# A two-block transformer kernel on one core: the order of the first loads, the place of the bias table, and four PSUM banks for the attention probabilities

## The reference

```
cs = silu(c)
mod = (cs @ ada_w[l] + ada_b[l]).reshape(B, 3, 3, D)            # shift, scale, gate
h = rmsnorm(x, norm_g[l, 0]) * (1 + mod[:, 0, 1]) + mod[:, 0, 0]
x = x + 0.5 * mod[:, 0, 2] * swiglu(h, w_gate[l, 0], w_up[l, 0], w_down[l, 0])
h = rmsnorm(x, norm_g[l, 1]) * (1 + mod[:, 1, 1]) + mod[:, 1, 0]
x = x + mod[:, 1, 2] * mixer(h, ...)
h = rmsnorm(x, norm_g[l, 2]) * (1 + mod[:, 2, 1]) + mod[:, 2, 0]
x = x + 0.5 * mod[:, 2, 2] * swiglu(h, ...)
```

```
logits = where(mask, q @ k.T * 64 ** -0.5 + bias, -1e30)
m = max(logits); p = exp(logits - m); s = sum(p)
o_g = p @ v / s ; lse_g = m + log(s)
o = sum_g softmax_g(lse)[g] * o_g
```

## Time and profile before

| | us |
|---|---|
| median of 3 runs | 3438.85 |
| lowest, highest | 3420.95, 3454.4 |
| the profiled execution's own time | 3429.66 |
| its span | 3427.9 |

### The profile page before, as it was taken

The page is one execution under the profiler, slowest core; times in us unless marked ns, Lnnn a source line. Parts: engine busy times, 40 slices in busy tenths (PEclk is TensorE's granted clock), DMA queues, the critical chain, the costliest instruction groups (busy, mean ns, idle before and its releaser), DMA issues.

```text
span 3427.9 us, 56270 instructions
## 1 busy us (share of the span) xinstructions
PE 3193.9 (93%) x24082; PEld 2691.2 (79%) x24083; DVE 1022.8 (30%) x2204; ACT 473.2 (14%) x1077; POOL 15.1 (0%) x26
## 2 busy tenths in 40 slices
PE   5999999999999999999998768997679999999998
PEld 4888888888888888888887757886666887668875
DVE  5213222320221322242035253368431111111113
ACT  1001112100100111210001200005320111101110
POOL 0000000000000000000000000000000000000000
PEclk8999999999999999999999669999889999999999
DMA  8646534364464563436446205760329788898884
GB/s 331 245 160 250 197 130 178 123 246 184 156 260 162 212 230 136 178 123 245 184 160 258 101 0 188 300 262 1 125 95 353 298 325 318 314 352 326 329 320 189
DMA packets 55190, 732.26 MB, mean 214 GB/s; under 512 B 6576, under 2 KB 6760, under 8 KB 10516
## 3 DMA queue, kind: packets, MB, share of 16 engines
q1 hardware_dynamic: 51092, 716.69, 54.7%
q0 software_dynamic: 3968, 13.74, 1.2%
HBM read 729.32 MB, written 4.23 MB: 214 GB/s over the span
## 4 chain that ended last, share of the span: by engine, by line
PE 81%; DMA 8%; DVE 7%; issue 2%; ACT 1%; SPq 0%; DVEq 0%; POOL 0%; ACTq 0%; POOLq 0%
PE psum L639 48%; PE psum L1041 11%; PE psum L1084 9%; PE psum L626 2%; PE psum L696 2%; DMA ring<-in_up_dram 2%; DMA ring<-in_up_e_dram 2%; DVE ring L1424 2%; PE psum L817 1%; PE psum L1065 1%; PE psum L1100 1%; DMA ring<-in_down_e_dram 1%; DMA ring<-in_w_qk_dram 1%; DVE work L1943 1%; DMA ring<-in_ada_dram 1%
## 5 line engine op out<-in xcount | busy, mean ns | idle before, releaser
L639 PE MATMUL psum<-h_t,ring 128*128 128x256 f32 x5888 | 1291.6, 382 | 31.2 <-DVE h_t L1570 8.8
L639 PEld LDWEIGHTS psum<-h_t,ring 128*128 128x128 f32 x5888 | 1124.3, 191 | 197.6 <-issue 29.0
L639 PE MATMUL psum<-work,ring 128*128 128x256 f32 x2752 | 603.4, 382 | 21.8 <-ACT work L1255 10.2
L639 PEld LDWEIGHTS psum<-work,ring 128*128 128x128 f32 x2752 | 526.7, 192 | 96.8 <-ACT work L1255 10.6
L1041 PE MATMUL psum<-h_t,ring 128*64 128x96 f32 x11264 | 471.7, 247 | 5.9 <-DMA ring<-in_up_e_dram 5.6
L1041 PEld LDWEIGHTS psum<-h_t,ring 128*64 128x64 f32 x11264 | 467.8, 137 | 9.1 <-issue 7.8
L1084 PE MATMUL psum<-ring,work 128*96 128x512 f32 x704 | 304.1, 593 | 0.6 <-DMA ring<-in_down_e_dram 0.5
L1424 DVE SCALAR_TENSOR_TENSOR ring<-ring,cond 128x1024 f32<-128x1024 f32 x240 | 279.2, 1220 | 36.5 <-DMA ring<-in_ada_dram 35.4
L1084 PEld LDWEIGHTS psum<-ring,work 128*96 128x96 f32 x704 | 114.1, 163 | 184.9 <-issue 183.1
L1487 DVE TENSOR_TENSOR work<-work,psum 128x256 f32<-128x256 f32 (+1 forms) x118 | 49.7, 421 | 624.2 <-PE psum L639 609.3
L2235 DVE TENSOR_TENSOR work<-work,psum 128x256 f32 x176 | 74.2, 421 | 403.8 <-PE psum L1041 403.8
(11 more groups left out here) (326 smaller groups left out, 1652.2 us busy)
## 6 DMA issues: line engine op xcount, KB each, us to landing
ring<-in_up_e_dram SPq DMA_DIRECT2D x64, 2048.0 KB, 7.7
ring<-in_ada_dram SPq DMA_DIRECT2D x60, 2048.0 KB, 7.8
ring<-in_up_dram SPq DMA_DIRECT2D x55, 2048.0 KB, 7.9
ring<-in_down_e_dram SPq DMA_DIRECT2D x32, 1792.0 KB, 8.5
ring<-in_down_dram SPq DMA_DIRECT2D x20, 2816.0 KB, 9.6
ring<-in_up_e_dram SPq DMA_DIRECT2D x32, 1536.0 KB, 8.4
ring<-in_down_e_dram SPq DMA_DIRECT2D x16, 2048.0 KB, 8.9
ring<-in_w_qk_dram SPq DMA_DIRECT2D x12, 2048.0 KB, 8.6
```

The lines of the kernel that those rows point to most:

```text
L639: mm = pe.matmul(half(b), w, moving(k, j * lin.groups + m), start=(k == 0), stop=(k == depth - 1))
```

## The change

- SyncE: the eight small inputs become a function that is called after the third modulation chunk of `ada0` has been issued; the fourth follows them.
- VectorE: no longer waits for the small inputs first and no longer copies x. It starts with the modulation products of three chunks, then adds the squares, then does the fourth chunk's products, then waits for the small inputs, adds the modulation's bias, prepares and scales the tiles. The bias row's add comes after the eight tiles, and the wait for `rows_out` after that.
- ScalarE: no longer waits for the small inputs ahead of silu(c), and copies x from the banks.
- `mix`: head n uses bank 4 + n % 4; before the first product TensorE waits for bank 6's two earlier reads, and then, head by head, for that head's copy. The counts in `stages` and in `combine` follow.

```diff
@@ -172,7 +172,7 @@
     ln_after = with_(ln, most_x=1)
     ln_along = with_(ln, x_summed=DT)
     logits = with_(uses(b4=4, b5=4), maxima=1, probs=HG, bias_in=16)
-    mix = uses(b4=4, b5=4, b6=1, b7=1)
+    mix = uses(b4=2, b5=2, b6=3, b7=3)
     prologue = {
         "load_x": with_(uses(b0=1, b1=1, b2=1, b3=1), cond_in=16, cond_set=1),
         "bias_rows": uses(b4=1),
@@ -534,12 +534,13 @@
         @block.sync
         def _(sp):
 
-            for dst, src in ((x_tok, dram["x"]), (ident[:, :], dram["ident"]), (vec[:, :], dram["vec"]),
-                             (one_hot, dram["one_hot"]), (off_mask, dram["off_mask"]),
-                             (table, dram["rel_bias"]),
-                             (bgate[:, :], dram["b_gates"]),
-                             (iota8[:, :], dram["iota8"])):
-                sp.dma_start(dst, src).then_inc(small_in, 16)
+            def small_inputs():
+                for dst, src in ((x_tok, dram["x"]), (ident[:, :], dram["ident"]), (vec[:, :], dram["vec"]),
+                                 (one_hot, dram["one_hot"]), (off_mask, dram["off_mask"]),
+                                 (table, dram["rel_bias"]),
+                                 (bgate[:, :], dram["b_gates"]),
+                                 (iota8[:, :], dram["iota8"])):
+                    sp.dma_start(dst, src).then_inc(small_in, 16)
 
             def stream(p):
                 def load(source, width):
@@ -551,6 +552,12 @@
                         sp.dma_start(ring[:, slot, 0:width], src).then_inc(chunk_in[slot], 16)
                     return chunk
 
+                if p.name == "ada0":
+                    for n in range(p.what.adas):
+                        load("ada", 32 * P)(n, 0, p.slot(n))
+                        if n == SLOTS - 1:
+                            small_inputs()
+                    return
                 walk(p, loop_on(sp), load(p.what.source, p.what.width), load("ada", 32 * P))
 
             def stream_rounds(p):
@@ -712,19 +719,17 @@
             def mix(p, g, lp):
 
                 for n in range(HG):
-                    b = 4 + n % 2
+                    b = LIN + n % LIN
                     pe.wait_ge(signal["probs"], lp.of("probs", n + 1))
-                    pe.wait_ge(bank_free[b], reads(p, b, n // 2))
+                    pe.wait_ge(bank_free[b], reads(p, b, n // LIN))
                     for c in range(3):
                         mm = pe.transpose(bank(b)[:, c * P:(c + 1) * P],
                                           logit[:, n, c * P:(c + 1) * P], ident[:, :])
                     mm.then_inc(signal[f"full{b}"], 1)
-                pe.wait_ge(bank_free[4], reads(p, 4, 4))
-                pe.wait_ge(bank_free[5], reads(p, 5, 4))
-                pe.wait_ge(bank_free[6], reads(p, 6))
-                pe.wait_ge(bank_free[7], reads(p, 7))
+                pe.wait_ge(bank_free[6], reads(p, 6, 2))
                 for n in range(HG):
                     e = (g * HG + n) * HD
+                    pe.wait_ge(bank_free[LIN + n % LIN], reads(p, LIN + n % LIN, n // LIN) + 1)
                     mm = pe.matmul(bank(6)[:, n * HD:(n + 1) * HD], prob_t[:, n, 0:P],
                                    vtok[:, 0, e:e + HD], start=True, stop=True)
                 mm.then_inc(signal["full6"], 1)
@@ -1204,14 +1209,18 @@
                 for b in range(LIN):
                     act.wait_ge(bank_free[b], reads(p, b))
                 for n in range(1, HG, 2):
-                    act.wait_ge(bank_full[5], products(p, 5, n // 2))
-                    act.activation(prob_t[:, n, :], bank(5)[:, 0:3 * P], ACT.Copy).then_inc(bank_free[5], 1)
-                act.wait_ge(bank_full[7], products(p, 7))
+                    b = LIN + n % LIN
+                    act.wait_ge(bank_full[b], products(p, b, n // LIN))
+                    act.activation(prob_t[:, n, :], bank(b)[:, 0:3 * P], ACT.Copy).then_inc(bank_free[b], 1)
+                act.wait_ge(bank_full[7], products(p, 7, 2))
                 act.activation(o_g[:, g, 1, :], bank(7), ACT.Copy).then_inc(bank_free[7], 1)
 
-            act.wait_ge(small_in, 128)
             act.wait_ge(signal["cond_in"], place("ada0").of("cond_in", 0))
             act.activation(cond[:, :], cond[:, :], ACT.Silu).then_inc(signal["cond_set"], 1)
+            p = place("load_x")
+            for b in range(LIN):
+                act.wait_ge(bank_full[b], products(p, b))
+                act.activation(x[:, 2 * b:2 * b + 2, :], bank(b), ACT.Copy).then_inc(bank_free[b], 1)
             for b in range(LIN):
                 act.wait_ge(bank_free[b], reads(place("norm0", 0), b))
             for l in steps.loop("layer", DEPTH):
@@ -1648,9 +1657,10 @@
                 for b in range(LIN):
                     dve.wait_ge(bank_free[b], reads(p, b))
                 for n in range(0, HG, 2):
-                    dve.wait_ge(bank_full[4], products(p, 4, n // 2))
-                    dve.tensor_copy(prob_t[:, n, :], bank(4)[:, 0:3 * P]).then_inc(bank_free[4], 1)
-                dve.wait_ge(bank_full[6], products(p, 6))
+                    b = LIN + n % LIN
+                    dve.wait_ge(bank_full[b], products(p, b, n // LIN))
+                    dve.tensor_copy(prob_t[:, n, :], bank(b)[:, 0:3 * P]).then_inc(bank_free[b], 1)
+                dve.wait_ge(bank_full[6], products(p, 6, 2))
                 dve.tensor_copy(o_g[:, g, 0, :], bank(6)).then_inc(bank_free[6], 1)
 
             def conv(p):
@@ -1674,8 +1684,8 @@
 
                 mx, sums, w, t = (att[:, k, :, :] for k in (0, 2, 3, 4))
                 over = lambda a: a.unsqueeze(1).to_broadcast([P, NG, TT * HG])
-                dve.wait_ge(bank_free[6], reads(mp, 6, 0) + 1)
-                dve.wait_ge(bank_free[7], reads(mp, 7, 0) + 1)
+                dve.wait_ge(bank_free[6], reads(mp, 6, 2) + 1)
+                dve.wait_ge(bank_free[7], reads(mp, 7, 2) + 1)
                 dve.tensor_tensor(t[:, 0, :], mx[:, 0, :], mx[:, 1, :], ALU.max).then_inc(dve_done, steps.one())
                 dve.wait_ge(dve_done, steps.count())
                 dve.tensor_tensor(t[:, 0, :], t[:, 0, :], mx[:, 2, :], ALU.max).then_inc(dve_done, steps.one())
@@ -1701,26 +1711,25 @@
                 dve.wait_ge(dve_done, steps.count())
                 dve.tensor_tensor(o_tok, o_tok, o_g[:, 2, :, :], ALU.add).then_inc(signal["mixed"], 1)
 
+            p = place("ada0")
+            dve.wait_ge(signal["cond_set"], p.of("cond_set", 0))
+            for n in range(p.what.adas):
+                if n == SLOTS:
+                    for f in range(1, DT - 1):
+                        squares_so_far(place("norm0", 0), f)
+                ada_sums(p)(n, 0, p.slot(n))
             dve.wait_ge(small_in, 128)
-            p = place("load_x")
+            ada_next(p, (new_shift_scale, *ada_b(0, 0, 2)))
+            prepare(vcol("norm_g", 0, DT))
             for b in range(LIN):
-                dve.wait_ge(bank_full[b], products(p, b))
-                dve.tensor_copy(x[:, 2 * b:2 * b + 2, :], bank(b)).then_inc(bank_free[b], 1)
+                dve.wait_ge(bank_free[b], reads(place("norm0", 0), b))
+            for f in range(DT):
+                raw_tile(f)
             p = place("bias_rows")
             dve.wait_ge(bank_full[4], products(p, 4))
             dve.tensor_tensor(bias_row[:, 0:383], psum[0:NG * HG, 4 * 512:4 * 512 + 383], off_mask,
                               ALU.add).then_inc(bank_free[4], 1)
-
-            for f in range(1, DT - 1):
-                squares_so_far(place("norm0", 0), f)
-            p = place("ada0")
-            dve.wait_ge(signal["cond_set"], p.of("cond_set", 0))
-            walk(p, loop(p), None, ada_sums(p))
-            ada_next(p, (new_shift_scale, *ada_b(0, 0, 2)))
             dve.wait_ge(rows_out, 16)
-            prepare(vcol("norm_g", 0, DT))
-            for f in range(DT):
-                raw_tile(f)
 
             for l in steps.loop("layer", DEPTH):
                 on = lambda name: place(name, l)
```

## The result

The changed kernel took 3411.72 us in the median (3402.97 to 3423.36, 11 runs) against 3434.78 us (3418.08 to 3454.4, 11 runs) for the kernel before: ratio 0.9936, 95% interval 0.9915 to 0.9957, so 22 us faster, between 15 and 29. Forecast were 12.6 us less and 3426 us. The time is in the range and the direction is right. The gain is larger than forecast, and the prologue's part of the change brought none of it (number 1). Of the 14.5 us between the forecast and the measured median, 4 are the starting point (the median of before was 3438.85 when the forecast was made, of three runs) and 10 are gain that was not forecast. Its profiled execution has a span of 3401.2 us, 26.7 less than that of before.

What follows compares the result with a forecast made beforehand. TensorE was taken as the bound (81% of the chain), so only its waits pay. Prologue 0 (1.5 us gained, 1.5 given back) plus 12.6 us from attention's six stages, off the median 3438.85, gave 3426 us; range 3405 to 3442.

Steps and rivals of the forecast that it cites:

- Attention, per stage: Six transposing stages of attention: four banks save 2.1 us each, 12.6 us in all (bounds 7 and 13).
- The eight waits at 0: Attention stages: eight more waits on TensorE's queue cost 0; at the other end 0.1 us each, 0.8 a stage.
- a gain beyond 2.2 is excluded: Attention: upper bound in us per transposing stage, since 24 transposes, one copy and their latencies fill 3.4 us.
- rival A: Attention: denser stages also end falls of TensorE's clock, 5 us more gained, 3421 us; chance 0.18.
- the likely case: The forecast itself, whole kernel: 12.6 us gained, 3426 us, no term for a changed clock; chance 0.55.
- Rival B: Attention's logits stages: more clock falls are added, 5 us each; four of six give 3446 us; chance 0.05.
- Prologue, first half: Start up to first weight matmuls: x lands at 25.0, TensorE starts at 40.1 against 41.6, 1.5 us gained.
- Prologue, second half: After the tiles: bias row's wait covered at 0, table transfer beside weight loads gives back 1.5 us.
- The wait at the bias row: VectorE, first block: mean square 1.6 us late at 48.0, costed at 0 because 5.9 us of slack cover it.
- the table transfer's cost: First block's up loads beside GpSimd's 3 MB table transfer: a 1.7 us wait, 1.5 new (bounds 0 and 5).
- the 2.2 us that I worked out for turns of equal size: First block: up weights' added delay if DMA engines gave both queues equal turns in bytes, instead of 1.5 us.
- Sum: Whole kernel: prologue 0 plus attention 12.6 us gained, 3426 us from the median 3438.85.

Runs made afterwards that it cites:

- number 1: Only the prologue's part of the change on the kernel before, attention still on two banks: 3426.27 us against 3424.62, ratio 1.0012.
- number 7: The changed kernel with TensorE waiting for all eight copies of a stage before the first product: 3416.27 us against 3426.7 for the kernel before, ratio 0.9965.
- 2: Only the four banks in attention's transposing stages, on the kernel before with its old prologue: 3407.96 us against 3424.62, ratio 0.9948.
- number 8: The kernel before with one unread filler product in each of three gaps between pairs of heads: 3420.65 us against 3426.7, ratio 0.9986.
- 4: The kernel before with GpSimd's table transfer issued later, near 130 us: 3423.52 us against 3426.7, ratio 0.9984.
- Number 5: The changed kernel with the table transfer late and the conditioning vector's load issued first on GpSimd: 3399.10 us against 3425.99 for the kernel before, ratio 0.9925.
- number 3: The changed kernel with GpSimd's table transfer issued later, near 130 us: 3406.78 us, ratio 0.9949 to the kernel before.

## Why the prediction was right, and where it was not

**Attention, per stage.** The chain of copies and transposes was laid out by the piece; forecast 2.1 us a stage, measured 2.2 to 2.4 (3.28 to 3.32 against 5.47 to 5.69). The products were to start at +3.50 and started at +3.28, since copies that follow each other at once overlap a little (two of VectorE's in 1.02 us, where I counted 0.56 each) and the fifth head's transposes wait less. The mechanism was right, 12.6 forecast against 13.7. The eight waits at 0 were right too (number 7). My bound "a gain beyond 2.2 is excluded" was slightly broken.

**The clock (rival A).** I gave it 5 us and a chance of 0.18, as a bet on one stage. It came in, with 4.3 us (5.6 in the profiles where the logits behind have the full clock), and numbers 2 and 8 support the cause that it names, within the limit said at number 8. Over the first stage of the first layer, three profiles with two banks and no filler (before, numbers 1 and 4) have the same picture, products 8.11 to 8.18 and logits 9.25 to 9.26 us. All the profiles with four banks have the products in 5.47 or 5.50. The step that failed is the weighing: the likely case kept the clock as it was, though the gaps that the change closes stood directly ahead of the fall. It was one stage of six, as rival A said. Rival B, added falls in attention, did not come.

**Prologue, first half.** x was named as what is late next, landing at 25.0; TensorE got it at 25.49. The adds were to end at 34.1 and ended at 33.3; weights at 40.1, measured 39.27; gained 2.3 instead of 1.5. Number 5 shows that x is the limit. What I had wrong was without effect: silu(c) was kept at 10.54 and ran at 13.97, because the vector, half a megabyte on GpSimd's queue, took 11.8 us beside the three large loads instead of 7.1. So VectorE's products started 3.4 us later than forecast, and the gap behind the twelfth was 1.68 us, not 8.

**Prologue, second half.** The wait at the bias row was covered, as predicted: mean square 47.34 (48.0 forecast), no gap before the next chunk. The mis-sized term is the table transfer's cost: 1.5 forecast. Set beside number 3, where only the table differs, the changed kernel is 2.0 us later at the third up chunk, 3.8 at the fifth and 4.3 late in the stage (ScalarE's L1167 at 141.71 against 137.44). The late landing itself was forecast well: 72.3, measured 72.5, which is 1.9 later than without the table. What was wrong is what TensorE makes of it. It wanted the load at 69.5 and not at 70.6, so it waited 3.1 and not 1.7, and the half clock behind the wait, 1.7, had no term at all.

I took the shares of DMA time from 32 to 47 us, 82 to 18, as the rule for where both queues flow, and it held: 81 to 17 between 60 and 67. By the Trainium skill ("DMA: Bandwidth & Descriptors", "Queues, rings and completion order") an engine takes the queues with work in turn, a packet each. Here the trace agrees roughly, in packets: 352 against 375 in the earlier trace rows, 149 against 109 between 60 and 67. In bytes the turns are unequal, since a packet is some 14 to 15 KB on SyncE's queue and 3 to 4 KB on GpSimd's (MB over packets in the same rows). So the 2.2 us that I worked out for turns of equal size was not the better number.

**Sum.** Forecast 0 for the prologue and 12.6 for the banks. Measured alone: 4 slower (1 faster to 9 slower) and 18 faster (12 to 24), together 22 and 18 in two comparisons. What the banks bring is 13.7 by the stages, and 18 in all leaves about 4, as much as the clock at the first stage gives in the profiles; the first comparison's 22 is a little more than the parts. That the forecast's range held it is in part luck: the range was set for the spread of the runs, and 10 us of the miss are gain that the likely case did not have. In the pair of profiles 2.9 us lie at the logits ahead of the first `mix`, and 8.5 behind the last one, most of it where the clock fell at other places: neither is claimed by a run.

## What to carry to other kernels

Where one engine fills buffers and two others empty them in lockstep, lay the chain out by the piece: more banks pay what the waits hold, and the same edit in the next such stage paid about as much again. Ask of idle gaps on TensorE what clock the stages behind them ran at, and give that a term of its own when you close them. And before reordering loads around a late one, find what shares the DMA engines with it: here one bulky transfer with over 200 us of slack (landed near 58 us, first read at 276) was the cause, and by the starts of the weight matmuls moving it alone did more than the reordering. When you read a queue's share over a stretch, look first whether the other queue had work in all of it.

## What the runs showed of the hardware

- The same products took 8.11 us behind gaps with TensorE busy for 3.36 of 5.69 us, and 5.50 us behind gaps filled to 4.62 of 5.51, with the granted clock at 0.66 and 1.00: work that nobody reads, on a waiting engine, made the kernel no slower. The first is so in three profiles, the second in one.
- One 3 MB copy from HBM to HBM on GpSimd's queue moved 2.22 MB in 8 us by itself (about 280 GB/s) and 0.43 MB in 7 us beside 2 MB loads on SyncE's queue (about 60 GB/s; 71 in the earlier trace rows). Its packets were as frequent as the loads' within a factor of 1.4, but of 3 to 4 KB against 14 to 15.
- A 0.5 MB load on GpSimd's queue, issued at 2.11 us in both kernels, landed in 7.1 us with the 2 MB loads of SyncE's queue issued from 4.54 on, and in 11.8 us with three of them issued from 1.37 to 2.73.
- After a wait of 3.11 us for a load, 128 matmuls took 29.57 us instead of 27.89, with the clock at 0.57 over the first 4 us.
